# One float32 DiT block pair on one NeuronCore: the last sums of the first FFN pass placed ahead of a weight's low part and of two modulation sections, and the recurrence's first values and masks loaded during the last projection tile

## The reference, cut to what matters

```python
def _conv_ffn(h, w_in, conv_w, conv_b, w_out, grid):
    u, g = jnp.split(h @ w_in, 2, axis=-1)
    g = _dwconv_grid(g, conv_w, conv_b, grid)
    return (jax.nn.silu(g) * u) @ w_out

# layer 0, after the pooling mixer: the FFN over x, then over the context
x = x + gt2 * _rms_norm(_conv_ffn(_modulate(x, ...), ...), norm_g[i, 3])
ctx = ctx + cgt2 * _rms_norm(_conv_ffn(_modulate(ctx, ...), ...), norm_g[i, 3])

# layer 1: z = h @ w_in gives q, k, v, the output gate o and four gate rows for 8 heads;
# the context's chunks (no output) set the state, then x's chunks are scanned,
# once forwards and once backwards:
s = jnp.einsum('bhctk,bhcsk->bhcts', q, k) * d_w
num = jnp.einsum('bhcts,bhcsv->bhctv', s, v) + a_t[..., None] * jnp.einsum('bhctk,bhckv->bhctv', q, c_prev)
h = num / jnp.maximum(jnp.abs(den), jnp.exp(-m_t))[..., None]
# (sigmoid(o) * (h_forwards + h_backwards)) @ w_out
```

## Time and profile before

| | |
|---|---|
| time, median of 3 runs | 2542.48 us (2542.19 to 2542.75) |
| the profiled execution: its time, its span | 2542.31 us, 2540.5 us |
| PE matmul busy | 2433.6 us, 96% of the span |
| DVE, ACT, POOL busy | 1496.7, 714.1, 622.1 us |
| chain that ended last | PE 88%, DVE 5%, DMA 2%, ACT 2%, issue 1% |
| TensorE's granted clock, mean | 0.983 |

### The profile page before, as it was taken

How to read it: one execution, slowest core, us unless ns; L and a number is a source line. 1 busy time by engine, 2 the same in 40 slices (tenths; PEclk the granted TensorE clock), 3 DMA queues, 4 the chain that set the end, 5 groups by cost and what they waited for, 6 DMA issues and landing times.

```text
span 2540.5 us, 35022 instructions
## 1 busy us (share of the span) xinstructions
PE 2433.6 (96%) x14154; PEld 1962.0 (77%) x14154; DVE 1496.7 (59%) x1612; ACT 714.1 (28%) x979; POOL 622.1 (24%) x207
## 2 busy tenths in 40 slices
PE   7989999999999989999999989798999999999997
PEld 5557777777777768998899978676677777777775
DVE  4466666666666664553533317714677666666776
ACT  3642211112111125553442233323211111111112
POOL 0012211122111234662221125500321222211222
PEclk9999999999999999999999989899999999999998
DMA  8552211222112243652121258323111111111103
GB/s 343 214 208 99 83 63 61 83 83 83 67 57 83 99 166 134 216 175 100 61 80 59 69 154 221 113 85 123 65 43 50 50 50 50 38 45 50 48 18 133
DMA packets 106250, 255.03 MB, mean 100 GB/s; under 512 B 8880, under 2 KB 62768, under 8 KB 91312
## 3 DMA queue, kind: packets, MB, share of 16 engines
q1 hardware_dynamic: 88592, 228.56, 26.1%
q10 hardware_dynamic: 17568, 25.17, 2.7%
HBM read 223.68 MB, written 30.02 MB: 100 GB/s over the span
## 4 chain that ended last, share of the span: by engine, by line
PE 88%; DVE 5%; DMA 2%; ACT 2%; issue 1%; SPq 0%; POOL 0%; ACTq 0%; DVEq 0%; POOLq 0%
PE ps L585 24%; PE ps L587 22%; PE ps L586 22%; PE ps L988 2%; PE ps L990 2%; PE ps L989 2%; PE ps L679 1%; DVE y_x L1961 1%; PE ps L1141 1%; PE ps L647 1%; PE ps L622 1%; PE ps L712 1%; PE ps L877 1%; PE ps L878 1%; PE ps L879 1%
## 5 line engine op out<-in xcount | busy, mean ns | idle before, releaser
L585 PE MATMUL ps<-hx_hi,w_hi 128*128 128x512 f32 x1552 | 615.3, 396 | 10.3 <-DVE hx_lo L2092 4.4
L586 PE MATMUL ps<-hx_lo,w_hi 128*128 128x512 f32 x1552 | 607.3, 391 | 0.0
L587 PE MATMUL ps<-hx_hi,w_lo 128*128 128x512 f32 x1552 | 607.1, 391 | 0.0
L1945 DVE SCALAR_TENSOR_TENSOR acc<-ps,fcv,acc 128x945 f32<-128x945 f32 (+2 forms) x352 | 430.1, 1222 | 266.0 <-ACT acc L1434 223.1
L2438 POOL TENSOR_TENSOR w_lo<-raw,w_hi 128x2048 fp32r<-128x2048 f32 x79 | 368.3, 4663 | 783.6 <-ACT w_hi L1386 355.9
L1961 DVE TENSOR_TENSOR y_x<-y_x,ps 128x1024 f32<-128x1024 f32 x336 | 409.9, 1220 | 117.7 <-PE ps L587 110.1
L585 PEld LDWEIGHTS ps<-hx_hi,w_hi 128*128 128x128 f32 x1552 | 293.0, 189 | 79.6 <-DVE hx_lo L2092 9.3
L587 PEld LDWEIGHTS ps<-hx_hi,w_lo 128*128 128x128 f32 x1552 | 293.1, 189 | 61.9
L586 PEld LDWEIGHTS ps<-hx_lo,w_hi 128*128 128x128 f32 x1552 | 293.4, 189 | 58.0
L2449 POOL TENSOR_TENSOR a_lo<-prod,a_hi 128x1024 fp32r<-128x1024 f32 x44 | 105.6, 2400 | 828.9 <-ACT a_hi L1452 828.9
L585 PE MATMUL ps<-a_hi,w_hi 128*128 128x512 f32 x704 | 292.1, 415 | 13.2 <-DVE y_x L1961 11.6
(11 more groups left out here) (295 smaller groups left out, 3350.9 us busy)
## 6 DMA issues: line engine op xcount, KB each, us to landing
raw<-in_ffn_w SPq DMA_DIRECT2D x66, 1024.0 KB, 5.2
raw<-in_ffn_w SPq DMA_DIRECT2D x66, 512.0 KB, 4.1
modw<-in_modw SPq DMA_DIRECT2D x48, 512.0 KB, 6.9
modw<-in_modw SPq DMA_DIRECT2D x24, 1024.0 KB, 4.9
raw<-in_mlstm_w SPq DMA_DIRECT2D x14, 1024.0 KB, 5.4
vch<-v_scr SPq DMA_DIRECT2D x18, 512.0 KB, 4.2
x_scr<-y_x ACTq DMA_DIRECT2D x32, 256.0 KB, 2.2
dmat<-row_scr SPq DMA_DIRECT2D x16, 512.0 KB, 5.7
```

The costliest lines, as they stand in the source:

```text
L585: pe.matmul(out, whi, hhi, start=first, stop=False)
L586: pe.matmul(out, whi, hlo, start=False, stop=False)
L587: return pe.matmul(out, wlo, hhi, start=False, stop=last)
L1945: dve.scalar_tensor_tensor(out, src, cv[:, t:t + 1], out, ALU.mult, ALU.add).then_inc(sem("tap_done"), 1)
```

## The change

Two places change. On DVE, the last tile's eight sums come right after the context's taps and gate; the low part of the context's first out weight stands ahead of the third sum, and the two modulation sections behind the eighth. On SP, the values of units 0 and 1 and the masks are issued right behind the out parts of the two weight tiles, before the waits for the last results of tile 11, and the wait for `state_zero` is gone. The rows of units 6 and 7 move behind `unit_done` of four and behind the values of units 4 and 5.

```diff
--- before.py
+++ after.py
@@ -505,11 +505,21 @@
             sp.wait_ge(sem("cols_ready"), 4)
             for K in (K_MOUT, K_MOUT + 1):
                 tile_out(K, a["mlstm_w"][K - K_MIN], K % 2)
+            def values_in(u):
+
+                sp.dma_start(vch[:, v_slot[u], :, 0:P], v_scr[units[u][1]].rearrange("p (h v) -> p h v", v=P))\
+                    .then_inc(sem(f"v_in{v_slot[u]}"), 16)
+
+            written = evac_of[len(MSEQ) - 2][-1] + 1
+            sp.wait_ge(sem("vo_done"), written)
+            for i in range(2):
+                sp.wait_ge(sem(f"stage_out{i}"), 16 * ((written + 1 - i) // 2))
+            values_in(0)
+            values_in(1)
+            sp.dma_start(masks[:], a["masks"]).then_inc(sem("mask_in"), 16)
             for i in range(2):
                 sp.wait_ge(sem(f"stage_out{i}"), run[i])
             sp.wait_ge(sem("vo_done"), len(evacs))
-            sp.wait_ge(sem("state_zero"), 2)
-            sp.dma_start(masks[:], a["masks"]).then_inc(sem("mask_in"), 16)
 
             def rows_in(u):
 
@@ -532,21 +542,20 @@
                         sp.wait_ge(sem("gated"), i - 1)
                     sp.dma_start(och[:, i % 2, :], o_scr[units[u][1] - 2]).then_inc(sem(f"o_in{i % 2}"), 16)
 
-            def values_in(u):
-
-                sp.dma_start(vch[:, v_slot[u], :, 0:P], v_scr[units[u][1]].rearrange("p (h v) -> p h v", v=P))\
-                    .then_inc(sem(f"v_in{v_slot[u]}"), 16)
-
-            for u in range(4):
-                if u < 2:
-                    values_in(u)
-                rows_in(x_units[u])
+            rows_in(x_units[0])
+            rows_in(x_units[1])
+            sp.wait_ge(sem("unit_done"), 4)
+            values_in(4)
+            values_in(5)
+            rows_in(x_units[2])
+            rows_in(x_units[3])
             for u in range(4, len(units)):
                 if u == 6:
                     sp.wait_ge(sem("unit_done"), 4)
                     sp.dma_start(mo_raw[:], a["mlstm_w"][len(MSEQ) + 2][:, 0:2048]).then_inc(sem("mo_in"), 16)
-                sp.wait_ge(sem("unit_done"), max(4, u - 1))
-                values_in(u)
+                if u >= 6:
+                    sp.wait_ge(sem("unit_done"), max(4, u - 1))
+                    values_in(u)
                 if u + 2 >= x_units[4] and u + 2 in x_index:
                     rows_in(u + 2)
                 gates_in(u - 1)
@@ -1927,7 +1936,7 @@
             def lo_tile(K):
                 lo_out(out_index(K) + 1, K % 2)
 
-            def ffn(p, y, between=None, ctx_root=None, ctx_part=None):
+            def ffn(p, y, between=None, ctx_root=None, ctx_part=None, in_last=None):
 
                 def conv(j, par, before_last=None):
                     s = (p.k0 + par) % 2
@@ -1951,8 +1960,10 @@
                     dve.wait_ge(sem("w_out_used"), j + (p.j0 + 1))
                     dve.tensor_tensor(prod[:, par, :], acc[:, 0:p.T], bank(2, p.T), ALU.mult).then_inc(sem("a_done"), 1)
 
-                def add(j, par):
+                def add(j, par, hook=None):
                     for d in range(KT):
+                        if hook is not None:
+                            hook(d)
                         if d < 7:
                             dve.wait_ge(sem("y_part"), j * 7 + (p.parts0 + d + 1))
                         else:
@@ -1981,7 +1992,7 @@
                 gate(FT - 1, 1)
                 if between is not None:
                     between()
-                add(FT - 1, 1)
+                add(FT - 1, 1, in_last)
 
             def ctx_taps(j):
 
@@ -2162,12 +2173,16 @@
 
                 ctx_taps(0)
                 ctx_gate(0)
-                lo_tile(K_FFNC)
-                dve.wait_ge(sem("mod_done"), 6)
-                derive(0, (0,), 0)
-                derive(0, (5,), 4)
-
-            ffn(p0, y_x, first_of_ctx, lambda: root("c_pre2", TC), ctx_split)
+
+            def in_last_sums(d):
+
+                if d == 2:
+                    lo_tile(K_FFNC)
+
+            ffn(p0, y_x, first_of_ctx, lambda: root("c_pre2", TC), ctx_split, in_last_sums)
+            dve.wait_ge(sem("mod_done"), 6)
+            derive(0, (0,), 0)
+            derive(0, (5,), 4)
             ctx_ffn()
```

## The result

The changed kernel takes 2524.07 us (median of four runs, 2520.68 to 2526.72) where the kernel before took 2542.44 (2542.19 to 2542.75): 0.9927 of it, with a 95% interval of 0.991 to 0.9944, or 18.4 us less. The forecast was 2525.7. The profiled execution took 2521.62 us.

A forecast was written before the change was run, and what follows sets the result against it. PE was taken to bound the kernel (88% of the chain), so savings count only where it stands still. 2542.3 - 9.1 - 7.5 = 2525.7 us; the range leaving out 2 in 10 was 2522.0 to 2531.5.

The forecast's parts named there:

- the first term: End of the first FFN pass: DVE's new order of sums gains 9.1 us, bounds 3.6 and 10.5.
- the second: Start of the recurrence: SP's new load order gains 8.0 - 0.5 = 7.5 us, bounds 4.5 and 9.
- signs of being wrong: Low part over 4 us; PE or DVE waiting for unit 6's matrix; unit 4's start to end changed over 2 us.
- the step of the low part: DVE, before the third sum: low part meets POOL's small operation, runs 1.1 us; PE stops again for 1.4 us.
- the upper bound of 10.5: End of the first FFN pass: low part meets no POOL operation, PE's second stop is nil, gain 10.5 us.
- The lock itself: DVE operations with both operands in SBUF wait for running POOL operations; sums with one from PSUM (1210 to 1223 ns) don't.
- rival (a): End of the first FFN pass: POOL's queued low part goes first, gain only 4.2 us, time 2530.6; chance 0.14.
- Behind the first stop: Context FFN: PE is busy 50.00 of 50 us there, so what is saved in the gap stays saved.
- rival (c): Context FFN held by its weights, saved time waited for elsewhere; only the second part left, 2534.8 us; chance 0.06.
- units 0 to 3: Start of the recurrence: unit 0's products start at 1496.9, fourth unit done at 1505.4, 8.0 us earlier.
- Unit 4's start: Recurrence: unit 4's products start between 1510.5 and 1511.5 instead of 1518.94, gain 8.0 us, bounds 7.0 and 8.9.
- The rows of units 6 and 7: Recurrence: rows issued behind values make unit 6's matrix late, a stall of 0.5 us, bounds 0 and 2.5.

The follow-up runs named there:

- low_later: Changed kernel with the low part ahead of the fourth sum instead of the third: 2529.16 us, 0.9955.
- sections_ahead: Changed kernel with the two modulation sections ahead of the sums again: 2533.89 us, 0.9973.
- pool_holds: Kernel before, with POOL's low part of the context's third tile waiting until the first of the last sums is done: 2537.49 us, 0.9991.
- low_ahead: Changed kernel with the low part ahead of all eight sums, the sections still behind them: 2529.83 us, 0.9948.
- loads_only: Kernel before with only SP's part of the change, DVE as before: 2532.76 us, 0.9962.
- sums_only: Kernel before with only DVE's part of the change, SP's queue as before: 2526.74 us, 0.9937.
- rows_old_place: Changed kernel with the rows of units 6 and 7 issued where they were before: 2529.1 us, 0.9953.
- both_again: The changed kernel timed once more, without an edit, against the kernel before: 2523.56 us, 0.9929.
- values_earlier: Changed kernel with the values of units 0 and 1 also ahead of the two weight tiles: 2524.03 us, 0.994.
- six_before: Changed kernel with SP's waits for the last o writes behind the rows, and unit 6's rows ahead of unit 4's values: 2523.51 us, 0.9931.

## Why the prediction was right, and where it was not

**The sum.** 16.6 us were forecast, 9.1 and 7.5; the profile has 16.8 at the two places, 10.0 and 6.8, and the medians differ by 18.4. Right in sum, with the first term 0.9 too small and the second 0.7 too large; that the two nearly cancel is luck. Two of the signs of being wrong that I had named came about even so: DVE waits for unit 6's matrix (1.07 us, without cost for PE), and from unit 4's start to the end it is 2.6 us less than before (1019.0 against 1021.6), 1.3 of them in the second FFN pass and 0.7 in the recurrence behind unit 7.

**First part, the step of the low part: mis-sized.** Less the 1.6 us by which this execution was ahead at gate 0 (936.00 less 934.40), I had POOL's small operation begin at 937.05 and DVE ask just behind it, at 937.2. POOL began at 937.08, but DVE asked at 937.00, in front of it. It ran 1.22 us without a wait, POOL's operation was stretched to 1.75 instead, and PE's second stop was 0.39, not 1.4. The gain is close to the upper bound of 10.5. All eight kernels with this order of DVE's have the same -10.0 in A. A request 1.8 us later meets POOL's next low part and loses 5.2 (low_later).

**The lock itself: right.** Operations with both operands in SBUF wait for POOL, sums with one in PSUM don't (336 sums, 1209 to 1224 ns after, as in the earlier trace rows). sections_ahead, low_later and pool_holds each show it from another side. The Trainium skill's sentence in "SBUF — State Buffer", "Who interferes with whom", that issue order decides who blocks, agrees with all three: 4.60 us against 1.22 for one and the same low part. So two engines can hold each other up with no semaphore between their operations.

**What I left out there: the clock behind a stop.** I named half clock as part of the 9.1, and gave it 1.2 us in rival (a). low_ahead puts it at 2.4, for a stop less than half as long as the one that the change removed. The price doesn't grow with the stop: behind the 9.66 us of before it was 1.5 (the gain of 10.0 less the 8.5 us by which PE stood still longer), and by the same sum it was 1.6 in low_later and pool_holds.

**Behind the first stop: right.** The context's gate 1 comes 11.59 us earlier than before, its gate 20 11.57, and the last copy to `stage` 11.51. Nothing is given back: rival (c) is out. Sections in DVE's idle time cost nothing (0.52 and 0.24 us ahead of 11.15 idle). In the second FFN pass 1.3 us more is gained. So it is (1.2 to 1.4 us) in all ten kernels whose modulation sections stand behind the sums, and in none of the three that have them ahead (loads_only, sections_ahead, pool_holds). I didn't foresee it, and no run shows how the one leads to the other.

**Second part, units 0 to 3: right to a tenth.** Shifted by the 11.5 us of what lies ahead, the forecast has the products of unit 0 at 1485.4 and the fourth unit done at 1493.9. The trace has 1485.31 and 1493.96 (1492.86 + 1.10), and SP issues unit 4's values at 1494.00.

**Unit 4's start: below the bound.** The forecast, so shifted, is 1499.4; the trace has 1500.82, a gain of 6.6 where the bounds were 7.0 and 8.9. Two sizes failed. The last write of o was taken at 1.85 us with one more microsecond at most; it takes 4.15 beside the early loads (4.43, 3.70 and 4.68 in other kernels with them), and SP, which waits for it, issues the rows 4.6 us behind the copy, not 2.3. The faster landing makes up for that, so that POOL's mask starts at 1492.66, 10.0 us after the copy, as before (10.1). And the scores of unit 5, which I had at 1.1 us, take 2.08: PE comes out of a stop of 4.26 us, and the granted clock from 1499 to 1501 is 0.50. The products follow at 0.50 too, with 3.51 us where 2.05 is what they take at the full clock (sums_only). The values, my first candidate for what would be late, are not what PE waits for.

**The rows of units 6 and 7: the sign was wrong.** I booked their move as a price of 0.5 us for a gain that came from the early values. The price is about right: DVE waits 1.07 us for unit 6's matrix, and PE doesn't.

```profile
1509.79 1.22 DVE L2320 TENSOR_TENSOR dmat<-dmat,ps 128x1024 f32<-128x1024 f32 x1 [1.07 <-ACT dmat L1784]
```

But rows_old_place shows that without the move there is no gain at all (-0.2): units 0 to 3 end as early and unit 4 then waits behind 12 row transfers. I had costed the new order against the old one as if unit 4's values would be issued at `unit_done` in either, and the old order doesn't do that once `unit_done` comes early.

**What the second part is worth is less certain than my figure.** All is measured against one profile of before. Two others with SP's old order, sums_only and pool_holds, are 3.1 and 2.7 us quicker in B, with unit 4's products at full clock. Against them the changed order gains 3.7 to 4.0 us, which fits the 3.2 by which both_again beats sums_only; loads_only alone, 9.8 under the kernel before, speaks for more. The two parts don't add up either: by medians they bring 15.8 and 9.8 us singly and 19.0 together. The 3.1 us of B that sums_only gains without any edit there is half of the 6.6 that are counted twice; the rest is open. Which of the two levels the kernel before usually has there is open: only its one profile could be read at this place.

## What to carry to other kernels

Look at which operation of another engine a slow tiny instruction runs beside before costing it: here two tiny additions, held for 4.4 us by POOL in front of sums that the bounding engine waits for, made up nearly half of a stop of 9.7, and behind such stops the blocks at half clock cost another 1.5 to 2.4 us. When a load is issued earlier, follow the queue on to the next load of the same kind: what stands between the two decides whether the gain survives. And lay the stages of several profiles against each other: here the one profile of before had a stage 3 us slower than its like.

## What was not expected of the hardware

- One low part of 128x1024 on DVE took 1.22, 3.43 and 4.60 us, as it was asked for 0.1 us ahead of the end of POOL's operation, 2.3 us ahead of it, or 1 us into the next one. POOL's small operation took 0.73 alone and 1.75 when DVE had gone ahead of it.
- A write of 128 KB to `o_scr` went from 1.85 us to between 3.23 and 6.19 when loads of values, weights and masks were under way, and from 5.86 on it held ACT's copies. SP's issue of one mask load took 3.25 us in that crowd, and 0.43 us where it came later (values_earlier).
- The same 16 products took from 2.05 us (sums_only, granted clock 1.00) to 3.51 (changed kernel, 0.50) and 3.81 (six_before). A short stop alone doesn't decide it: the 2.05 stand behind a wait of 2.55 us, the 3.81 behind one of 0.70. What else does is open.
